# Attention steps in pairs, spatial weights a tile later, and a zero block that opens the value bank

## What is computed

```python
def in_proj(h, w_in, ...):                      # h = rms_norm(x) * g, one projection
    q, k, v, gate_a, f_logit, u, vb, gate_b, g_a, g_b = split(h @ w_in)
    q, k = rms_norm(q), rms_norm(k)             # 8 heads of 64
    logf = log_sigmoid(f_logit + b_forget)
    u = gelu(u); vb = rms_norm(gelu(vb)) * v_norm_g
# prompt attention, causal, c = cumsum(logf):
s = q @ k.T * scale + (c[q] - c[k]);  attn = softmax(s) @ v
# the new tokens attend to 256 cached rows of their own and to themselves
# spatial gating, chunks of 128 rows, 8 groups of 64 columns:
s_sgu = tril(w_s) @ vb + b_s
a = attn * silu(gate_a);  b = u * s_sgu * silu(gate_b)
m = sigmoid(g_a) * (a @ w_pa) + sigmoid(g_b) * (b @ w_pb)
x = x + m @ w_o
```

## Time and profile before

| | |
|---|---|
| median of 3 runs | 2015.58 us (2014.07 to 2018.64) |
| the profiled execution | 2014.72 us, span 2013.0 us |
| busy: PE / DVE / ACT / POOL | 1919.7 (95%) / 973.0 (48%) / 672.8 (33%) / 511.7 (25%) us |
| mean granted clock of PE | 0.981 of full speed |
| transfers | 178.39 MB, 89 GB/s |
| first attention / spatial stage on PE | about 82 to 532 / 532 to 623 us |
| second attention / spatial stage on PE | about 1072 to 1523 / 1523 to 1613 us |

### The profile page before, as it was taken

The page is one execution under the profiler, slowest core; times in us unless marked ns, Lnnn a source line. Parts: engine busy times, 40 slices in busy tenths (PEclk is TensorE's granted clock), DMA queues, the critical chain, the costliest instruction groups (busy, mean ns, idle before and its releaser), DMA issues.

```text
span 2013.0 us, 30982 instructions
## 1 busy us (share of the span) xinstructions
PE 1919.7 (95%) x11188; PEld 1762.0 (88%) x11188; DVE 973.0 (48%) x2298; ACT 672.8 (33%) x1487; POOL 511.7 (25%) x523
## 2 busy tenths in 40 slices
PE   5999899999898999999999999999998999999998
PEld 4999898999877889998789988999997788999986
DVE  5546556554165334545445565656532643454431
ACT  5344344444133222113224344444432332231120
POOL 3623233332021112211135242333320211131010
PEclk7999999999999999999999999999999999999999
DMA  5231313123215222524324113131321253226151
GB/s 155 65 101 48 83 50 97 49 73 87 68 38 145 75 83 81 194 82 156 104 57 120 45 46 97 42 95 48 95 69 55 52 155 94 62 74 224 49 177 52
DMA packets 217803, 178.39 MB, mean 89 GB/s; under 512 B 50260, under 2 KB 191076, under 8 KB 217652
## 3 DMA queue, kind: packets, MB, share of 16 engines
q1 hardware_dynamic: 217652, 176.41, 30.4%
HBM read 131.65 MB, written 44.71 MB: 88 GB/s over the span
## 4 chain that ended last, share of the span: by engine, by line
PE 76%; DVE 9%; issue 5%; DMA 3%; ACT 3%; SPq 1%; POOL 1%; POOLq 0%; ACTq 0%; DVEq 0%
PE bank L76 21%; PE bank L77 20%; PE bank L78 20%; PE bank L1306 2%; PE bank L1319 2%; PE bank L2071 1%; PE bank L1289 1%; PE bank L1320 1%; PE bank L1291 1%; PE bank L2094 1%; DVE at_prob L1186 1%; DVE at_ptlo L1202 1%; PE bank L1266 1%; DVE sg_sT L1534 1%; DMA me_stage<-in_w_proj_b 1%
## 5 line engine op out<-in xcount | busy, mean ns | idle before, releaser
L76 PE MATMUL bank<-keep_hhi,at_fhi 128*128 128x384 f32 (+1 forms) x768 | 260.2, 339 | 3.3 <-ACT at_th L954 3.3
L77 PE MATMUL bank<-keep_hlo,at_fhi 128*128 128x384 f32 (+1 forms) x768 | 253.5, 330 | 0.0
L78 PE MATMUL bank<-keep_hhi,at_flo 128*128 128x384 f32 (+1 forms) x768 | 253.4, 330 | 0.0
L76 PE MATMUL bank<-aw_whi,keep_hhi 128*128 128x384 f32 (+3 forms) x576 | 198.3, 344 | 1.9 <-POOL aw_wlo L252 1.2
L76 PE MATMUL bank<-keep_hhi,bw_whi 128*128 128x384 f32 (+1 forms) x576 | 196.3, 341 | 0.5 <-DVE br_th L1958 0.5
L77 PE MATMUL bank<-aw_wlo,keep_hhi 128*128 128x384 f32 (+3 forms) x576 | 195.7, 340 | 0.0
L78 PE MATMUL bank<-aw_whi,keep_hlo 128*128 128x384 f32 (+3 forms) x576 | 195.7, 340 | 0.0
L1000 ACT ACTIVATE at_prob<-at_prob,at_nmx 128x128 f32<-128x128 f32 (+7 forms) x128 | 99.5, 777 | 280.1 <-DVE at_nmx L1193 279.8
L77 PE MATMUL bank<-keep_hlo,bw_whi 128*128 128x384 f32 (+1 forms) x576 | 189.4, 329 | 0.0
L78 PE MATMUL bank<-keep_hhi,bw_wlo 128*128 128x384 f32 (+1 forms) x576 | 189.1, 328 | 0.0
L1202 DVE TENSOR_TENSOR at_ptlo<-bank,at_pthi 128x512 fp32r<-128x512 f32 x192 | 106.2, 553 | 156.7 <-ACT at_pthi L1010 156.7
(11 more groups left out here) (252 smaller groups left out, 4398.1 us busy)
## 6 DMA issues: line engine op xcount, KB each, us to landing
at_stage<-in_w_in SPq DMA_DIRECT2D x160, 128.0 KB, 2.5
mg_gate<-gates SPq DMA_DIRECT2D x32, 544.0 KB, 5.2
gates<-at_th SPq DMA_DIRECT2D x64, 192.0 KB, 2.4
br_stage<-in_w_in SPq DMA_DIRECT2D x40, 256.0 KB, 3.3
at_stage<-in_w_in SPq DMA_DIRECT2D x48, 192.0 KB, 2.6
at_decay<-ncum SPq DMA_DIRECT2D x16, 512.0 KB, 3.9
br_k<-in_cache_k SPq DMA_DIRECT2D x32, 256.0 KB, 3.1
br_v<-in_cache_v SPq DMA_DIRECT2D x32, 256.0 KB, 3.1
```

The lines of the kernel that those rows point to most:

```text
L76: nc.tensor.matmul(out, sh, mh, start=start and i == 0, stop=False)
L77: nc.tensor.matmul(out, sh, ml, start=False, stop=False)
L78: last = nc.tensor.matmul(out, sl, mh, start=False, stop=stop and i == n - 1)
```

## The change

In attention two steps are taken at a time: `T T`, reads, `V V` (and `O`), then the score steps due with a projection or a filler half between them, then loads and splits (`N`, `W`, `Y`), then filler. Transposes `X` that are due move to the head of the next pair. The spatial weights are transposed after tile 2, with the first gating directly behind; ACT's and DVE's copies of them and DVE's gating follow a tile later; the norm gain has a semaphore of its own, and the bias loads come after those of `wb`. The product that opens `vps` takes a block of zeros that POOL writes in the spatial phase, and comes first in step `D`; DVE's memset of `own_p` is gone.

```diff
--- before.py
+++ after.py
@@ -136,6 +136,7 @@
     g.kpg = Region(nc, "br", g.me_at)("k", [P, NK, NPG, WA])
     last = g.kpg[:, NK - 1, 0, :]
     g.above, g.ones, g.nub = last[:, 0:P], last[:, P:2 * P], last[0:64, 2 * P:2 * P + 64]
+    g.zeros = last[0:64, 3 * P:4 * P]
 
 
 def load_pair(sp, g, l, p, k, out, done):
@@ -691,21 +692,30 @@
     first = fill.at
     total = sum(2 * (s[0] == "Z") for v in after.values() for s in v) + len(fill.pieces) - first
     spent = 0
-    for n in range(len(steps) + LAG):
-        if n < len(steps):
-            plan.append(("T",) + steps[n])
+    turned = []
+    for n in range(0, len(steps) + LAG, 2):
+        due = after.pop(n, []) + after.pop(n + 1, [])
+        plan += turned
+        turned = [s for s in due if s[0] == "X"]
+        scores = [s for s in due if s[0] == "S"]
+        projections = [s for s in due if s[0] == "Z"]
+        plan += [("T",) + s for s in steps[n:n + 2]]
         fill.read(0)
-        if n >= LAG:
-            plan.append(("V",) + steps[n - LAG])
-            h, G, j = steps[n - LAG]
+        for h, G, j in steps[max(0, n - LAG):n - LAG + 2]:
+            plan.append(("V", h, G, j))
             if j == 4 * G + 3:
                 plan.append(("O", h, G))
-        for s in after.pop(n, []):
-            if s[0] == "Z":
+        while scores or projections:
+            if scores:
+                plan.append(scores.pop(0))
+            if projections:
                 fill.before_z()
                 spent += 2
-            plan.append(s)
-        while spent + fill.at - first < total * (n + 1) / (len(steps) + 1) and fill.at < len(fill.pieces):
+                plan.append(projections.pop(0))
+            elif scores:
+                fill.half()
+        plan += [s for s in due if s[0] in "NWY"]
+        while spent + fill.at - first < total * (n + 2) / (len(steps) + 1) and fill.at < len(fill.pieces):
             fill.half()
     fill.end()
     assert not after
@@ -1362,8 +1372,8 @@
     w_in = [S(f"win{i}") for i in range(NST)]
     w_hi, w_lo = S("whi"), S("wlo")
     pt_in, l_in = S("pt"), S("lp")
-    cst, cst2, ws_in, wb_z, ws_m, ws_ps, ws_hi, ws_lo, wb_ps, wb_r = (S(x) for x in (
-        "cst", "cst2", "ws", "wbz", "wsm", "wsps", "wshi", "wslo", "wbps", "wbr"))
+    gvb_in, gvb_r, cst, cst2, ws_in, wb_z, ws_m, ws_ps, ws_hi, ws_lo, wb_ps, wb_r = (S(x) for x in (
+        "gvbin", "gvb", "cst", "cst2", "ws", "wbz", "wsm", "wsps", "wshi", "wslo", "wbps", "wbr"))
     z_ready, sq_r, w3_r, th_r, g2_r, ss_r, ms_r, rs_r, vb_r, vh_r, vl_r, g_ps, g_r, out = (S(x) for x in (
         "z", "sq", "w3", "th", "g2", "ss", "ms", "rs", "vb", "vh", "vl", "gps", "gr", "out"))
 
@@ -1374,16 +1384,16 @@
     def _(sp):
         all_through(sp, g)
         sp.dma_start(ws[:, :, :], g.w_s[bass.ds(l, 1), :, :, :].rearrange("a g t s -> t (a g) s")).then_inc(ws_in, 16)
-        sp.dma_start(gvb[:, :], g.v_norm_g[bass.ds(l, 1), :].to_broadcast([P, WA])).then_inc(cst, 16)
-        for p in range(PAIRS):
-            for hh in range(2):
-                sp.dma_start(bs[HD * hh:HD * hh + HD, p, :],
-                             g.b_s[bass.ds(l, 1), 2 * p + hh, :].to_broadcast([HD, P])).then_inc(cst, 16)
+        sp.dma_start(gvb[:, :], g.v_norm_g[bass.ds(l, 1), :].to_broadcast([P, WA])).then_inc(gvb_in, 16)
         sp.dma_start(g.pages[:, :], g.page_table[:, :]).then_inc(pt_in, 16)
         sp.wait_ge(wb_z, 1)
         for b in range(DB):
             sp.dma_start(wb[DT * b:DT * b + DT, :, DT * b:DT * b + DT],
                          g.w_s[bass.ds(l, 1), :, 0:DT, 0:DT].rearrange("a g t s -> t (a g) s")).then_inc(cst2, 16)
+        for p in range(PAIRS):
+            for hh in range(2):
+                sp.dma_start(bs[HD * hh:HD * hh + HD, p, :],
+                             g.b_s[bass.ds(l, 1), 2 * p + hh, :].to_broadcast([HD, P])).then_inc(cst, 16)
         for u in range(PRE_BRANCH):
             if u >= NST:
                 sp.wait_ge(w_lo, u - NST + 1)
@@ -1410,11 +1420,11 @@
     @block.scalar
     def _(act):
         all_through(act, g)
-        act.wait_ge(cst, 144)
-        nc.scalar.activation(gvb[:, :], gvb[:, :], ACT.Copy, scale=0.5).then_inc(ws_m, 1)
+        act.wait_ge(gvb_in, 16)
+        nc.scalar.activation(gvb[:, :], gvb[:, :], ACT.Copy, scale=0.5).then_inc(gvb_r, 1)
         for t in range(NT):
             n = ROWS[t]
-            if t == 1:
+            if t == 2:
                 for i in range(2):
                     act.wait_ge(ws_ps, i + 1)
                     nc.scalar.activation(w_hi_s[:, 4 * i:4 * i + 4, :],
@@ -1463,6 +1473,7 @@
         def constants(part):
             if part == 0:
                 link(nc.gpsimd.memset(ones, 1.0))
+                link(nc.gpsimd.memset(g.zeros, 0.0))
 
                 link(nc.gpsimd.affine_select(out=above, in_=ones, compare_op=ALU.is_gt, fill=0.0, base=0,
                                              pattern=[[-1, P]], channel_multiplier=1))
@@ -1544,10 +1555,10 @@
             last.then_inc(g_r, 1)
 
         all_through(dve, g)
-        dve.wait_ge(ws_m, 2)
+        dve.wait_ge(gvb_r, 1)
         for t in range(NT):
             n = ROWS[t]
-            if t == 1:
+            if t == 2:
                 for i in range(2):
                     dve.wait_ge(ws_hi, i + 1)
                     nc.vector.tensor_tensor(w_lo_s[:, 4 * i:4 * i + 4, :], wps[i][:, :].rearrange("p (g t) -> p g t", g=4),
@@ -1559,8 +1570,10 @@
             if t:
                 dve.wait_ge(vl_r, min(t, PT_))
             nc.vector.scalar_tensor_tensor(g2[0:n, :], thv[0:n, :], 1.0, z, ALU.add, ALU.mult).then_inc(g2_r, 1)
-            if t:
-                gating(t - 1)
+            if t == 2:
+                dve.wait_ge(cst, 16 * H)
+            if t >= 2:
+                gating(t - 2)
             dve.wait_ge(ss_r, t + 1)
             nc.vector.tensor_scalar(ms[0:n, :], ss[0:n, :], 1.0 / WA, EPS, ALU.mult, ALU.add).then_inc(ms_r, 1)
             dve.wait_ge(rs_r, t + 1)
@@ -1570,13 +1583,14 @@
                 dve.wait_ge(vh_r, t + 1)
                 nc.vector.tensor_tensor(vl[:, t % 2, :], g2[:, :], vh[:, t % 2, :].bitcast(F32),
                                         ALU.subtract).then_inc(vl_r, 1)
+        gating(NT - 2)
         gating(NT - 1)
         dve.drain().then_inc(g.dve_through, 1)
 
     @block.tensor
     def _(pe):
         def spatial_weights():
-            pe.wait_ge(ws_m, 2)
+            pe.wait_ge(ws_m, 1)
             for i in range(2):
                 for k in range(4):
                     last = nc.tensor.transpose(wps[i][:, k * P:(k + 1) * P], ws[:, 4 * i + k, :], g.ident[:, :])
@@ -1633,9 +1647,9 @@
                 last = three(nc, zps[t % 2][0:n, :],
                              [(g.h_hi[:, k, r], g.h_lo[:, k, r], hi, lo)], k == 0, k == KT - 1)
             last.then_inc(z_ready, 1)
-            if t == 1:
+            if t == 2:
                 spatial_weights()
-            elif t:
+            if t >= 2:
                 gating(t - 2)
         first_piece(0)
         gating(NT - 2)
@@ -1875,7 +1889,7 @@
                     act.wait_ge(w_used, blk + 1)
                 nc.scalar.activation(hi_of(u), stage[:, slot(u), :], ACT.Copy).then_inc(w_hi, 1)
             elif s[0] == "D":
-                act.wait_ge(fills, 2)
+                act.wait_ge(fills, 1)
                 for p in range(PAIRS):
                     for hh in range(2):
                         r = slice(HD * hh, HD * hh + HD)
@@ -1934,7 +1948,6 @@
         for s in plan:
             if s[0] == "M":
                 all_through(dve, g)
-                nc.vector.memset(own_p[:, :, :], 0.0).then_inc(fills, 1)
                 nc.vector.memset(qbd[:, :, :, :], 0.0).then_inc(fills, 1)
             elif s[0] == "W":
                 u = s[1]
@@ -2016,14 +2029,13 @@
             if s[0] == "D":
                 pe.wait_ge(zq, 1)
                 pe.wait_ge(*pages_in)
+                nc.tensor.matmul(vps[:, :], g.zeros, selb[:, :, :].rearrange("p b n -> p (b n)"),
+                                 start=True, stop=False)
                 nc.tensor.matmul(dps[0:64, 0:P], g.lp[:, 0, :], above, start=True, stop=False)
                 nc.tensor.matmul(dps[0:64, 0:P], g.lp[:, 1, :], ones, start=False, stop=True)
                 nc.tensor.matmul(dps[0:64, P:2 * P], g.lp[:, 1, :], above, start=True, stop=True)
                 nc.tensor.matmul(dps[0:H, PAST:PAST + 64], g.logf[0:NS_TOK, PT_, :], nub,
                                  start=True, stop=True).then_inc(d_ps, 1)
-                pe.wait_ge(fills, 1)
-                nc.tensor.matmul(vps[:, :], g.v_s[:, 0:P], own_p[:, :, :].rearrange("p b n -> p (b n)"),
-                                 start=True, stop=False)
             elif s[0] == "P":
                 i, half = s[1:]
                 if i < 3:
```

## The result

The changed kernel took 2003.08 us (median of 5 runs, 2001.68 to 2009.88), the kernel before 2015.58 in the same rounds (2013.71 to 2021.49). The ratio is 0.9941, 95% interval 0.9927 to 0.9955: faster by 12.5 us, 0.6%. The forecast was 28.2 us faster, 1987.4. The time lies inside the range, whose upper part was there for rival 2 and its spread, but less than half of the gain came.

The account below looks back on a forecast made before the run. PE, busy 95% of the span, was taken to bound the kernel, so only its idle time and low clock could yield. Gains of 11.9 (attention), 11.6 (spatial) and 4.7 us (opener) summed to 28.2: 1987.4 us, range 1964 to 2005.

Parts of the forecast that it names:

- rival 2: Attention gives nothing, paced by weight transfers and other bunched reads; only spatial stage and opener gain, 16.3 us: 1999; chance 0.22.
- Removed waits, 30.1 us: Attention, both layers: PE's waits for score banks 13.9, last half head's output 12.9 and ACT's bank reads 3.3 us all vanish.
- New waits, 23.8 us: Attention: the new order makes PE wait 11.9 us per layer at newly listed places, 23.8 us in all.
- P 5 0 0: Attention, filler block 5: a bank read on ACT stands behind weight splits paced by transfers; new wait 5.2 us per layer.
- P 7 1 0: Attention, one pair of heads later: a bank read again stands behind weight splits on ACT; new wait 2.0 us per layer.
- the late decay loads: Attention, heads 2, 4 and 6: decay load behind a projection on SP's queue delays DVE and ACT; 1.4 + 0.9 us per layer.
- S 3 6 and S 5 6: Attention: two score steps with only 1.6 us of other steps before them, right after a projection; 0.5 us wait each.
- the first head: Attention: its score steps are normalised one by one, delaying a bank read by 1.4 us per layer.
- Clock, 9.8 gained and 6.2 lost: Attention: four low-clock stretches vanish, gaining 9.8 us; the two new 5.2 us waits lower the clock, costing 6.2.
- Spatial, 11.6: Spatial stage, both layers: transposing spatial weights a tile later removes waits, leaving a new 2.8 us wait each; 11.6 us gained.
- Opener, 4.7: Opener to first key page: no wait for DVE's memset, key page next late; 2.4 and 2.3 us gained, 4.7 in all.
- Of the rivals, the first: Attention: late decay loads block PE at three heads in two layers and lower the clock; 2032; chance 0.07, part or whole.

Follow-up runs that it names:

- changed, first / second profile: The changed kernel itself, profiled in two runs: first one of 2009.88 us, slowest of its five, then one of 2003.13 us.
- attention plan alone: Only the paired attention steps (`attention_plan`) put into the kernel before: 2022.87 us, ratio 1.0036 to the kernel before.
- reads first: Changed kernel with the bank reads that are due put ahead of a filler block's weight splits: 1982.18 us, ratio 0.9841 to the kernel before.
- decay first: Changed kernel with the next head's decay load issued ahead of the projection: 1989.65 us, ratio 0.9874 to the kernel before.
- both: Changed kernel with bank reads ahead of weight splits and the decay load ahead of the projection: 1971.45 us, ratio 0.9776 to the kernel before.
- both, no half-chunk between: Changed kernel with bank reads and decay load moved ahead, half-chunks between score steps moved later in the pair: 1982.88 us, ratio 0.9832 to the kernel before.
- both, splits spread: Changed kernel with bank reads and decay load moved ahead, next projection's weight splits two per pair over four pairs: 1963.41 us, ratio 0.9738.

## Why the prediction was wrong

The two attentions of each profile, worked out from PE's matmuls, in us: length, idle time, work at the low clock, and the length less idle time and less 0.46 of that work.

| kernel | length | idle | at low clock | rest |
|---|---|---|---|---|
| before | 967.7 | 31.6 | 21.5 | 926.2 |
| changed, first / second profile | 976.9 / 972.9 | 39.2 / 38.0 | 24.5 / 18.7 | 926.5 / 926.3 |
| attention plan alone | 975.5 | 38.3 | 23.5 | 926.4 |
| reads first | 953.8 | 23.5 | 6.8 | 927.1 |
| decay first | 959.5 | 28.3 | 14.1 | 924.8 |
| both | 941.3 | 15.7 | 3.4 | 924.1 |
| both, no half-chunk between | 956.1 | 22.2 | 23.2 | 923.3 |
| both, splits spread | 933.9 | 10.8 | 0 | 923.1 |

The lengths differ by up to 43 us, the rest by 4.0. So idle time and the clock explain nearly all of it, and what went wrong is in the terms on them:

- *Removed waits, 30.1 us*: right at nearly all their places. For the score banks the half-chunk experiment shows by what; for the last half head's output (12.9 us) no run varies the filling by itself, and the profile shows only that the waits are gone. One, at S 4 5, stayed with about 1 us a layer, counted below.
- *New waits, 23.8 us*: **the step that failed**. They came to 36.3 us (mean of the two profiles, both layers): P 5 0 0 10.8 (forecast 10.4, right); P 7 1 0 6.6 (4.0); the late decay loads 7.0 (4.6); S 3 6 and S 5 6 3.4 (2.0); the first head 3.4 (2.8); and two sets that I had not listed, S 4 5 2.1 and P 14 0 0 with P 15 1 0 3.0. The mechanisms that I named were all there; I followed the reads behind splits at two places of four and sized each place alone, with the steps ahead of it taken as on time, while moving the decay loads alone took P 5 0 0 from 5.4 to 4.7 us a layer.
- *Clock, 9.8 gained and 6.2 lost*: I charged only the two waits of 5.2 us. Those of 2.3 to 3.7 us at P 7 1 0 and S 6 2 brought it down in one or both layers too, as one of 2.65 us had in the earlier trace rows. Worked out with the same 0.46, the change of the clock is -1.4 and +1.3 us in the two profiles, so nothing, where I had 3.6. (The 0.33 and 0.17 us of the earlier trace rows make 0.48 rather than 0.46, and the fit below 0.41; on some 20 us of work that is 1 us.)
- *Order on PE, 2 us*: nothing; the last column is 926.2 before and 926.3 to 926.5 after.
- *Attention in sum*: +11.9 forecast; -9.2 and -5.2 in the profiles, and -7.2 in all when timed alone. The three terms account for 19.9 of the 21.1 us missed in the first profile and 16.3 of the 17.1 in the second.
- *Spatial, 11.6*: right in its waits, too small as a term. Idle went from 18.1 to 7.4 us over both layers, 10.7 where I had 11.6, with the new wait 3.45 instead of 2.8 us. The stage is 15.6 us shorter all the same; 4 us of this come only with the paired plan, which lets SP start sooner, as the prediction said (without it the stage gained 11.6 us). Over the 10.7 us of idle time, part is the clock (13.6 us of low stretches before, 10.2 after, up to 1.6 us). Part is that a wait costs more than its gap: before, gating and the next projection started 2.11 us apart with a gap of 0.41, now 1.43 us apart without one, thus 0.27 us on top of each gap; if the same holds at all 12 waits for `sg_g` and `sg_vl` that are gone, 3 us (an estimate). The Trainium skill's fit in *DMA: Bandwidth & Descriptors*, "Anatomy of one DMA", would have had the gain's load land in 2.6 us and the wait at 1.2 us (estimates from the page); the load landed after 4.3 and 4.5 us in this profile, the wait came to 3.45 us, and the measurement decides.
- *Opener, 4.7*: 3.3 and 3.8, the key page being the next thing late, as said.

Of the rivals, the first was right in kind: late decay loads do hold PE. Its price was off. Their removal is worth 13 us over six places, 2.2 us each, less than the 4.7 a place at which the change would have come out slower, and more than the sum's 0.8. The second, 1999 with attention at nothing, came nearest in time, and the bunched reads that it spoke of are there (P 14 0 0 and P 15 1 0, not followed, and P 7 1 0, underrated); but attention did not come to nothing, it lost. That attention alone would turn slower I gave no chance of its own; the sum's attention term had a margin of 11.9 us on 23.8 us of new waits, and they grew by half.

## What to carry to other kernels

When an order is rewritten, walk every in-order queue through the new one and mark each entry that waits for a transfer or for a freed buffer; whatever another engine needs soon must stand ahead of it, and such entries must not follow in a bunch as long as the ring of buffers. Here two small edits of the plan made the difference between 6 us lost and 26 gained by pairing. A forecast that nets many small waits should assume that the list of new ones is incomplete, and count each with the clock that it can bring down.

## What the runs showed that was not expected

A fit over the 28 attentions of the 14 profiles (with a small term each for the layer and for the number of waits) gives 1.12 us of length per us of idle time and 0.41 per us of work at the low clock, with misses under 0.6 us in all but one (1.5). By which waits are counted, the first figure is 1.06 to 1.17. Gaps read from a trace thus understate somewhat what removing a wait is worth here. And a mended wait paid twice, by the clock: the edit of the reads removed 15.7 us of idle time from the two attentions (39.2 in the first profile of the changed kernel, 23.5 with it) and 17.7 us of work at the low clock (24.5 to 6.8); from the second profile it is 14.5 and 11.9. With 10.8 us of idle time, in waits of 1.2 us and less, none was left, though in the kernel before one began at 118.40 in the earlier trace rows, after a wait of 1.36 us and within one of 0.69.
